# Values shifted by one row through device memory, and a late weight tile's low pieces two steps later

## The reference

```
kv = _rms(x, kv_norm) @ w_kv;  k, v = split(kv)
q, g = split(_rms(x, b_norm) @ w_in)
z = q . k * scale
log_beta = log_sigmoid(z);  log_1mb = where(kpos < qpos, log_sigmoid(-z), 0)
suffix = reverse_cumsum(log_1mb) - log_1mb
a = where(kpos < qpos, exp(log_beta + suffix), 0)
out = x + (a @ v * silu(g)) @ w_out
```

## Time and profile before

| | |
|---|---|
| runs | 2459.96, 2457.83, 2457.62 us |
| profiled execution, its own time | 2457.59 us |
| its span in the trace | 2455.8 us |
| PE busy | 2281.5 us (93%) |
| DVE busy | 1512.5 us (62%) |
| ACT busy | 952.0 us (39%) |
| mean granted TensorE clock | 0.975 of full |

### The profile page before, as it was taken

How to read it: one execution, slowest core, us unless ns; L and a number is a source line. 1 busy time by engine, 2 the same in 40 slices (tenths; PEclk the granted TensorE clock), 3 DMA queues, 4 the chain that set the end, 5 groups by cost and what they waited for, 6 DMA issues and landing times.

```text
span 2455.8 us, 29670 instructions
## 1 busy us (share of the span) xinstructions
PE 2281.5 (93%) x12574; PEld 1159.9 (47%) x12574; DVE 1512.5 (62%) x1959; ACT 952.0 (39%) x1396; POOL 203.4 (8%) x246
## 2 busy tenths in 40 slices
PE   7999999999999999999999789999997339998999
PEld 5445444444444444445444566544443114655655
DVE  6898857776667757787422799755342021765762
ACT  5245335322222323433323887423230011665750
POOL 0001030000000003533101000120000000000000
PEclk9999999999999999999999999999998669999999
DMA  5110001111110111121210100211301000001021
GB/s 182 35 69 35 1 35 38 65 61 43 69 69 35 37 68 68 37 104 52 81 40 1 35 1 1 104 35 69 137 30 59 26 25 34 1 1 35 1 86 52
DMA packets 51732, 120.16 MB, mean 49 GB/s; under 512 B 2650, under 2 KB 8339, under 8 KB 51216
## 3 DMA queue, kind: packets, MB, share of 16 engines
q1 hardware_dynamic: 48616, 105.40, 12.1%
q10 hardware_dynamic: 2984, 12.87, 1.3%
HBM read 101.49 MB, written 12.58 MB: 46 GB/s over the span
## 4 chain that ended last, share of the span: by engine, by line
PE 77%; DVE 10%; DMA 8%; ACT 4%; issue 1%; ACTq 0%; SPq 0%; DVEq 0%
PE PS L72 72%; DMA OV<-R 6%; PE PS L75 5%; ACT RG L81 2%; DVE R L93 2%; DVE RG L101 1%; DVE R L101 1%; DVE RG L104 1%; DMA RG<-in_a_w_in 1%; ACT R L81 1%; DVE scl L110 1%; DVE oss L110 1%; DVE RG L107 1%; DVE dg L104 1%; DVE mx L110 0%
## 5 line engine op out<-in xcount | busy, mean ns | idle before, releaser
L72 PE MATMUL PS<-R,RG 128*128 128x512 f16 (+1 forms) x5568 | 1205.5, 378 | 103.0 <-DVE R L101 98.5
L72 PEld LDWEIGHTS PS<-R,RG 128*128 128x128 f16 (+1 forms) x5568 | 554.2, 104 | 747.0 <-DVE R L101 86.7
L72 PE MATMUL PS<-RG,R 128*128 128x512 f16 (+2 forms) x3080 | 604.6, 363 | 3.0 <-DVE R L93 2.5
L72 PEld LDWEIGHTS PS<-RG,R 128*128 128x128 f16 (+1 forms) x3080 | 281.0, 106 | 301.4 <-issue 18.5
L101 DVE SCALAR_TENSOR_TENSOR RG<-RG,scl 128x4096 f16<-128x4096 f32 (+2 forms) x70 | 213.2, 3053 | 101.3 <-ACT RG L81 101.3
L81 ACT ACTIVATE RG<-RG,scl 128x4096 f16<-128x4096 f32 (+2 forms) x70 | 177.8, 2556 | 232.3 <-DVE scl L113 232.3
L107 DVE TENSOR_TENSOR_SCAN RG<-RG,dg 128x128 f32<-128x128 f32 (+7 forms) x128 | 167.0, 1346 | 100.2 <-ACT RG L81 99.9
L101 DVE SCALAR_TENSOR_TENSOR R<-PS,scl,R 128x512 f32<-128x512 f32 (+1 forms) x211 | 148.6, 743 | 115.8 <-PE PS L72 109.2
L110 DVE TENSOR_REDUCE scl<-RG 128x1 f32<-128x4096 f32 (+1 forms) x35 | 150.3, 4293 | 99.7 <-DMA RG<-in_w_ff 41.4
L122 POOL PARTITION_ALL_REDUCE scl<-scl x49 | 34.6, 709 | 1727.9 <-DVE scl L110 1447.9
L75 PE MATMUL PS<-ident,RG 128*128 128x128 f32 x864 | 148.7, 287 | 25.6 <-DVE RG L107 15.5
(11 more groups left out here) (141 smaller groups left out, 1675.0 us busy)
## 6 DMA issues: line engine op xcount, KB each, us to landing
RG<-in_w_ff SPq DMA_DIRECT2D x16, 2048.0 KB, 8.5
RG<-in_a_w_in SPq DMA_DIRECT2D x8, 2048.0 KB, 8.9
xspill<-R ACTq DMA_DIRECT2D x2, 4096.0 KB, 15.3
RG<-in_w_kv SPq DMA_DIRECT2D x4, 2048.0 KB, 8.0
RG<-in_b_w_in SPq DMA_DIRECT2D x4, 2048.0 KB, 7.9
RG<-in_w_in SPq DMA_DIRECT2D x3, 2048.0 KB, 8.4
R<-in_x SPq DMA_DIRECT2D x8, 512.0 KB, 7.9
RG<-in_w_out SPq DMA_DIRECT2D x2, 2048.0 KB, 7.8
```

Source lines behind the costliest of these rows:

```text
L72: return self.engine.matmul(*a, **k) if self.engine else Nothing()
```

## The change

Values: after ACT has copied both halves of token tile t, it also issues a DMA that writes the tile to a new buffer in device memory, `vs` (1024 x 1024, rows in token order). In the query stage the moved tile is then read from that buffer, with rows starting one earlier, into the same two buffers: one DMA of 128 rows, where there were one of 127 rows and one of a single row. For t = 0, which has no row before it, 127 rows are read in two DMAs of 15 and 112 rows. The first read waits for all eight writes. Pieces: in DVE's program the low half of piece y stands in step y + 2.

```diff
+        vs = nc.dram_tensor("vspill", [S, D], F32, kind="Internal").ap()
...
-                if z in sb_pieces:
-                    s = w_slot(40)
-                    e.wait_ge(*sig("w_high").at(40, z))
-                    low_half(piece(s, z), piece(s[:, 4096:8192], z), piece(w_raw(40), z), w_col(40, 2)).then_inc(
-                        *(sig("weight").up(40) if z == sb_pieces[-1] else step.up()))
+                if z - 2 in sb_pieces:
+                    s, y = w_slot(40), z - 2
+                    e.wait_ge(*sig("w_high").at(40, y))
+                    low_half(piece(s, y), piece(s[:, 4096:8192], y), piece(w_raw(40), y), w_col(40, 2)).then_inc(
+                        *(sig("weight").up(40) if y == sb_pieces[-1] else step.up()))
...
+                e.wait_ge(*sig("bank_act").at("v2", 1, t))
+                e.dma_start(vs[128 * t:128 * t + 128, :], V2[:, t, :]).then_inc(*sig("v_out").up(by=16))
...
                         before, done = V2_BEFORE[t % 2], sig(f"v_before{t % 2}")
-                        e.wait_ge(*sig("bank_act").at("v2", 1, NT - 1))
                         e.wait_ge(*sig("h_low").at("b_norm_2", 1, 7))
                         if t < 6:
                             e.wait_ge(*sig("v_steps").at(t + 2))
+                        e.wait_ge(*sig("v_out").last())
                         if t:
-                            e.dma_start(before[0:1, :], V2[127:128, t - 1, :]).then_inc(*done.up(t, 0, by=16))
-                        e.dma_start(before[1:128, :], V2[0:127, t, :]).then_inc(*done.up(t, by=16))
+                            e.dma_start(before, vs[128 * t - 1:128 * t + 127, :]).then_inc(*done.up(t, by=16))
+                        else:
+                            e.dma_start(before[113:128, :], vs[112:127, :]).then_inc(*done.up(t, 1, by=16))
+                            e.dma_start(before[1:113, :], vs[0:112, :]).then_inc(*done.up(t, by=16))
```

## The result

| | before | changed |
|---|---|---|
| median | 2457.72 us (4 runs, 2454.65 to 2459.96) | 2321.91 us (4 runs, 2318.97 to 2323.93) |
| profiled execution | 2457.59 us | 2318.97 us |
| span in the trace | 2455.8 us | 2317.2 us |
| mean granted clock | 0.975 | 0.999 |

The ratio is 0.9447, with a 95% interval from 0.9431 to 0.9464: 135.8 us faster. The forecast was 2325 us, with a range from 2317 to 2339.

The account below looks back on a forecast made before the run. PE, busy 93% of the span, was taken as the bound, so only closing its holes or lifting its clock counts. 2457.6 less 112.5 (shift) less 19.5 (pieces) gave 2325.6, stated as 2325 us, range 2317 to 2339.

Parts of the forecast that it names:

- The place and the order of dependence: Query stage: PE waits eight times for DVE's low half, queued behind a subtraction that waits for the slow moved copy.
- The shift, 112.5 us: Query stage, PE's stretch 1877.42 to 2025.00: 111.2 us less for seven products, plus 1.3 for the clock, if no wait stays.
- The price of a read, 4 us: Query stage: one 512 KB moved tile read from device memory takes 4 us, chosen between 2.4 and 7.9.
- The schedule built on it: Query stage: low half of product 9 at about 1892, PE needing its bank at 1908.6, so 16 us to spare.
- The claimed limit of 6.3 us per read: Query stage: with reads one after another, the schedule holds up to a pace of 6.3 us per read.
- The writes, zero: Values stage: the eight added writes cost PE zero, at most 1 us, and the wait for all eight costs nothing.
- The bound of up to 5 us for an issue: Values stage, ACT's queue: issuing one write costs about 0.4 to 5 us.
- The pieces, 19.5 us: Attention steps 28 to 35: DVE no longer waits for ACT's piece; 19.9 us go, 15.5 certain, 19.5 taken.
- Half-good reads: Query stage: reads keep a pace of 8 us, PE stands up to 12 us; 2340 us, chance 0.09.
- The rival of slow writes: Values stage: writes also run on one engine, 20.2 us each, so the first read lands late; 2488 us, chance 0.02.
- The rival that the pieces do nothing: Attention: ACT's own queue, not the wait for the piece, holds DVE's scans; 2345 us, chance 0.06.
- The signs that the prediction named for being right: Queries: no PE hole, subtractions 2 to 8 us apart, last before 1892, reads over 100 GB/s; attention: no piece waits.

Follow-up runs that it names:

- Experiments 2 and 3: Changed kernel with reads cut into 127 and 1 rows: 2434.08 us; changed kernel with SBUF-to-SBUF copies of 112, 15 and 1 rows, no device memory: 2320.57 us.
- the first experiment: Two kernels, each one part of the change on the kernel before: shift through device memory alone, 2340.95 us; low pieces two steps on alone, 2434.18 us.
- experiment 5: Changed kernel with each read but the last tile's cut in two: 124 and 4 rows, 2322.31 us; 122 and 6 rows, 2348.52 us.
- experiment 6: Kernel before with only the eight writes to device memory and the wait for them added, nothing reading them: 2455.37 us against 2455.45.
- experiments 2 and 7: Changed kernel with reads cut into 127 and 1 rows, 2434.08 us; changed kernel with the eight writes cut so, reads whole, 2390.18 us.
- experiment 4: Changed kernel with the low pieces one step on instead of two: 2319.56 us, ratio 0.9448.
- experiment 1: Each part alone against the kernel before: shift through device memory, 2340.95 us, ratio 0.9529; low pieces two steps on, 2434.18 us, ratio 0.9903.

## Why the prediction was right

**The place and the order of dependence.** The order was slow copy, subtraction, low half, bank, product. Experiments 2 and 3 restore or remove the first link alone, and the whole hole comes or goes with it.

**The shift, 112.5 us.** The trace gives 112.9, the shift alone 117.2 between medians. The bound was read from PE's own window, so the only open question was whether a wait of PE stays; none did.

**The price of a read, 4 us.** No row of before had it; it was chosen between 2.4 and 7.9. The median landing was 4.7 us, with the load of tile 39 beside some of the reads, and 4.3 in the first experiment. The schedule built on it ran 5 us ahead of the forecast: the low half of product 9 was expected at 1892 and came at 1883.0, which is 1886.5 with the 3.5 us by which this execution was ahead. DVE did wait, 6.6 us in three waits, and the slack took it. The claimed limit of 6.3 us per read was between what experiment 5 showed harmless and harmful.

**The writes, zero.** Shown by experiment 6. The bound of up to 5 us for an issue, taken from the old copies, was not met: 0.33 us. The old issues are not an exception: experiments 2 and 7 have them as long, and each time DMAs of 127 rows are under way. In the kernel before even the mask's load of 64 KB, behind the last copy, took 4.35 us to issue, in the changed kernel 0.36.

**The pieces, 19.5 us.** 20.5 in the trace, 24.0 between medians; the reasoning by step lengths gave 19.9, and 0.4 were taken off for a remainder that did not exist. The lengths were also taken to the end of a step's last matmuls, 4.74 us for the first, where the next step starts 0.07 us sooner (4.67 from 2075.85 to 2080.52 above); over eight steps that is the 0.6 between 20.5 and 19.9. Two steps were not needed; one was enough (experiment 4).

**The rivals.** Half-good reads were priced at 2340 for a pace of 8 us; the pace of 9.7 gave 2348.5. The rival of slow writes was mis-sized: it charged them only through the wait of the first read, and put at 16.4 us each the point from which they, with slow reads, turn the result. Experiment 7, with reads fast, shows them to take ACT's time from the values stage on, some 28 us more than that way of counting gave. With slow reads as well it wasn't tried. The rival that the pieces do nothing, 2345 us, fell with experiment 1: alone they gained 24.0 us.

The signs that the prediction named for being right came too: the subtractions start 1.7 to 7.7 us apart and the last at 1884.8, the first reads are issued at 1845.3, and 512 KB in the median 4.7 us are 112 GB/s.

The forecast was 3 us above the median. The profiled execution was 6.6 us below the sum: 3.5 ahead of the change, 1.7 a clock dip in before's trace, and 1.4 in the two terms.

## What to carry to other kernels

When a copy runs at one flat, low rate for its whole length, look at the number of rows that its DMA has before its route: a shift by one row makes 127 out of 128, and here that alone kept the copy at 26 GB/s, some 20 us where 4 to 5 are enough; cutting it into 112 + 15 + 1 rows, or reading 128 rows from a buffer where an offset of one row is free, repairs it. Work on the side that one engine hands to another should be taken up a step later than it is made, behind what the step's main chain waits for. And a hole of the bounding engine can be priced from its own window, products in it times the pace outside; the estimate of the rest then only has to say whether a wait remains.

## What the runs showed of the hardware that was not expected

- Issuing a DMA can hold the issuing engine's program: 0.33 us for a write of 128 rows, up to 29.3 us for a pair of 127 and 1 rows with earlier ones still in flight, and the activation behind it idle all that time. Pairs of 122 and 6 or 124 and 4 rows took 0.57 and 0.59 us, so a slow transfer in flight isn't enough for it; where issues were long, DMAs of 127 rows were under way.
- A copy that runs on few engines delays a transfer of another queue that runs on all. The four 2 MB loads of this weight land in 7.9 us as a median. That of tile 39 took 20.9 us in the kernel before, beside the old copies, 10.8 beside the fast reads, 21.1 beside reads of 127 rows, 21.0 beside 122 and 19.3 beside 124. In the kernel before it was issued at 1858.1 and ran at 347 to 394 GB/s for some 5 us, and from then to its landing at 1879.0 the rate was that of the old copies alone, 23 to 27 GB/s. So most of it had moved early and a small rest landed late; that this rest shares the copy's one engine is likely, but was not tried apart.
- The route through SBUF or device memory makes little difference to the shift of a tile: 4.0 us as a median for its part of 448 KB in the one, 4.7 us for 512 KB in the other, and 2320.57 against 2321.91 us for the kernel.
